# Attention values taken per unit instead of per pair of heads, with five buffers for turned weights instead of six

## The reference

```python
o_cmp = einsum(masked_softmax(q k_cmp^T), v_cmp)   # 31 compressed keys
o_sel = einsum(masked_softmax(q k_sel^T), v_sel)   # causal, branch 0 in the kernel
o_win = einsum(masked_softmax(q k_win^T), v_win)   # causal, branch 1
o = g0 * o_cmp + g1 * o_sel + g2 * o_win           # 16 heads of 64, 4 groups of keys
return o @ w_out
```

## Time and profile before

| | |
|---|---|
| median of 3 runs | 1592.23 us (1592.12 to 1593.16) |
| the profiled execution's own time | 1593.16 us |
| its span, first to last instruction | 1591.4 us |
| PE busy over the span | 1527.1 us (96%) |
| DVE, ACT, POOL busy | 1109.3, 689.9, 309.6 us |
| granted PE clock, mean | 0.99 of full speed |

### The profile page before, as it was taken

The page is one execution under the profiler, slowest core; times in us unless marked ns, Lnnn a source line. Parts: engine busy times, 40 slices in busy tenths (PEclk is TensorE's granted clock), DMA queues, the critical chain, the costliest instruction groups (busy, mean ns, idle before and its releaser), DMA issues. The chain is left out here.

```text
span 1591.4 us, 20732 instructions
## 1 busy us (share of the span) xinstructions
PE 1527.1 (96%) x8107; PEld 1258.5 (79%) x8107; DVE 1109.3 (70%) x1607; ACT 689.9 (43%) x1175; POOL 309.6 (19%) x237
## 2 busy tenths in 40 slices
PE   4898999999999999989999999999999999999998
PEld 3687898888888897867777888888888987766677
DVE  6688888898889763359885685656634814788775
ACT  3432552322314544337774541322233524778551
POOL 0122112233222000039872011111100011000210
PEclk9899999999999999989999999999999999999999
DMA  9575246669575314230000255433432231211101
GB/s 332 201 249 185 80 152 238 232 199 329 197 273 180 106 32 157 89 105 2 2 1 28 80 200 170 145 134 122 142 106 93 71 109 66 78 67 53 54 1 53
DMA packets 106743, 203.33 MB, mean 128 GB/s; under 512 B 6025, under 2 KB 11414, under 8 KB 106646
## 3 DMA queue, kind: packets, MB, share of 16 engines
q1 hardware_dynamic: 106646, 202.01, 36.9%
HBM read 199.90 MB, written 2.10 MB: 127 GB/s over the span
## 5 line engine op out<-in xcount | busy, mean ns | idle before, releaser
L722 ACT ACTIVATE WH<-RAW 128x2048 fp32r<-128x2048 f32 (+1 forms) x112 | 210.1, 1886 | 362.1 <-DMA RAW<-in_ff_w_in_dram 218.9
L1219 DVE TENSOR_TENSOR WL<-RAW,WH 128x2048 fp32r<-128x2048 f32 (+1 forms) x107 | 276.5, 2604 | 128.9 <-ACT WH L722 128.1
L486 POOL PARTITION_ALL_REDUCE MROW<-MACC x30 | 142.2, 4740 | 596.9 <-DVE MACC L1253 511.3
L2055 PE MATMUL PS<-WH,HIDh 128*128 128x512 f32 (+1 forms) x576 | 218.4, 379 | 5.9 <-DVE HIDl L1537 4.9
L2055 PE MATMUL PS<-WL,HIDh 128*128 128x512 f32 (+1 forms) x576 | 218.2, 379 | 0.0
L2055 PE MATMUL PS<-WH,HIDl 128*128 128x512 f32 (+1 forms) x576 | 218.2, 379 | 0.0
L2055 PE MATMUL PS<-HTh,WH 128*128 128x512 f32 (+1 forms) x520 | 202.4, 389 | 0.0
L2055 PE MATMUL PS<-HTl,WH 128*128 128x512 f32 (+1 forms) x520 | 202.4, 389 | 0.0
L2055 PE MATMUL PS<-HTh,WL 128*128 128x512 f32 (+1 forms) x520 | 202.3, 389 | 0.0
L1253 DVE SCALAR_TENSOR_TENSOR MACC<-MRAW,CS,MACC 128x512 f32<-128x512 f32 x182 | 136.9, 752 | 9.2 <-DMA MRAW<-in_ada_w_dram 1.0
L2012 PE MATMUL PS<-HTh,WH 128*128 128x256 f32 (+1 forms) x384 | 124.8, 325 | 6.7 <-ACT SG L1098 2.5
(11 more groups left out here) (325 smaller groups left out, 2935.2 us busy)
## 6 DMA issues: line engine op xcount, KB each, us to landing
MRAW<-in_ada_w_dram SPq DMA_DIRECT2D x46, 1024.0 KB, 7.3
RAW<-in_ff_w_in_dram SPq DMA_DIRECT2D x32, 1024.0 KB, 5.3
RAW<-in_ff_w_out_dram SPq DMA_DIRECT2D x32, 1024.0 KB, 5.0
RAW<-in_w_in_dram SPq DMA_DIRECT2D x16, 1024.0 KB, 5.3
MRAW<-in_w_ada_dram SPq DMA_DIRECT2D x12, 1024.0 KB, 9.0
RAW<-in_a_w_in_dram SPq DMA_DIRECT2D x8, 1024.0 KB, 9.7
MRAW<-in_kv_ada_w_dram SPq DMA_DIRECT2D x8, 1024.0 KB, 6.1
RAW<-in_kv_w_dram SPq DMA_DIRECT2D x6, 1024.0 KB, 5.1
```

The source lines that it names most:

```text
L486: pool.partition_all_reduce(MROW[:], MACC[:], P, RADD).then_inc(m_red, 1)
L722: act.activation(WH[:, wslot(u), 0:width(u)], RAW[:, u % 4, 0:width(u)], ACT.Copy).then_inc(w_hi, 1)
L1219: dve.tensor_tensor(WL[:, u % 4, 0:width(u)], RAW[:, u % 4, 0:width(u)], WH[:, wslot(u), 0:width(u)].bitcast(F32), ALU.subtract).then_inc( ...
L2055: mm = pe.matmul(po, a, b_, start=(k == 0 and i == 0), stop=(k == KT - 1 and i == len(ops) - 1), skip_group_check=len(ops) > 3)
```

## The change

`values` goes unit by unit: at i = 3 it takes the units i = 1, 3 and 2, and at i = 6 the units 4, 6 and 5. Each unit belongs to one head, and all its matmuls come one after the other. The near tile of head 0 (unit 2) is thereby multiplied at i = 3 and no longer at i = 6. Each stage now has 10 matmuls; before it was 8 and 12 where S is even and 6 and 14 where it is odd. Which matmuls there are does not change.

PT is a ring of five buffers over the rows of all superunits, so that a copy waits for the `values` that read the row five before it. The copy of i = 5 goes from ACT to DVE. The constants MD, IDB and MCM lie behind the PT, PBC and PTC buffers in on-chip memory, where the sixth PT was, and no longer ahead of them.

```diff
+    PT = [scratch(f"PT{i}", [P, 512]) for i in range(5)]
 ...
     MD, IDB = scratch("MD", [P, P], BF16), scratch("IDB", [P, P], BF16)
     MCM = scratch("MCM", [P, TT, 32], BF16)
 ...
-        return PT[row(u) % 6] if u % PER else PTC[u // PER % 2]
+        return PT[row(u) % 5] if u % PER else PTC[u // PER % 2]
 ...
-        return u % PER not in (3, 6)
+        return u % PER in (0, 1, 2, 4)
 ...
-        return 3 * (u // PER) + (1, 2, 3, 2, 3, 3, 3)[u % PER]
+        return 3 * (u // PER) + (1, 2, 2, 2, 3, 3, 3)[u % PER]
 ...
-        return u - PER if u % PER else u - 2 * PER
+        if u % PER == 0:
+            return u - 2 * PER
+        r = row(u) - 5
+        return PER * (r // 6) + r % 6 + 1 if r >= 0 else -1
 ...
-                pairs = ((1, 0, (u - 2, u)),) if i == 3 else ((1, 1, (u - 2, u)), (0, 0, (u - 4, u - 1)),
-                                                              (0, 1, (u - 4, u - 1)))
-                for blk, br, of in pairs:
-                    for kt in range(qts[blk] + 1):
-                        c_ = P * kt + (P * (qts[0] + 1) * br if blk == 0 else 0)
-                        for h in range(2):
-                            mm = pe.matmul(head(blk, h), VT[:, br, kt, HD * g:HD * g + HD],
-                                           turned_of(of[h])[:, c_:c_ + P], start=False,
-                                           stop=(br == 1 and kt == qts[blk]), skip_group_check=True)
+                for v in (u - 2, u, u - 1):
+                    S, i, pair, qts, blk, br, e, L = unit(v)
+                    for at_, br_ in parts(v):
+                        for kt in range(qts[blk] + 1):
+                            c_ = at_ + P * kt
+                            mm = pe.matmul(head(blk, e), VT[:, br_, kt, HD * g:HD * g + HD], turned_of(v)[:, c_:c_ + P],
+                                           start=False, stop=(br_ == 1 and kt == qts[blk]), skip_group_check=True)
```

More of the change, by code:

```diff
@@ L187, in program @@
     VC = scratch("VC", [P, GROUPS, 2 * HD])
+    assert w_at[0] <= o_w + 16384
+    w_at[0] = o_w + 16384
+    PT = [scratch(f"PT{i}", [P, 512]) for i in range(5)]
+    PBC = [scratch(f"PBC{i}", [P, P]) for i in range(2)]
+    PTC = [scratch(f"PTC{i}", [P, 2 * P]) for i in range(2)]
     MD, IDB = scratch("MD", [P, P], BF16), scratch("IDB", [P, P], BF16)
     MCM = scratch("MCM", [P, TT, 32], BF16)
[L191 to L195, removed]
     second = [at(n, [P, 4, T], F32, o) for n, o in (
```

## The result

| | before | after |
|---|---|---|
| median | 1592.47 us (1592.12 to 1593.16, 4 runs) | 1609.22 us (1606.83 to 1609.85, 4 runs) |
| ratio | | 1.0102, 95% interval 1.0085 to 1.0119 |
| profiled execution, span | 1593.16, 1591.4 us | 1608.31, 1606.6 us |

The change costs 16.7 us by the medians and 15.2 us by the two profiled spans. The forecast was 1614.4, in a range of 1600 to 1619: the right way and inside, but by the medians the loss is a quarter smaller than the forecast 22.2 us. Each ratio further down is taken against runs of the kernel before from the same session as the experiment (medians 1593.14 us for e1 to e4, 1593.19 for e5 to e8, 1593.01 for e9 and e10).

The account below looks back on a forecast made before the run. PE was taken to bound the attention: +24.4 us for values in one-head runs, less 1.3 and 0.9 us gained back, made +22.2 us, a median of 1614.4 us (chance 55%). Range 1600 to 1619 us, its own 1612 to 1619.

Parts of the forecast that it names:

- PE sets the pace, and values of one head take twice the time: Attention body: PE bounds; one head's matmul alone takes 0.218 us, and two of different heads share that time.
- One slot saved at each change of head, +24.4 us: Stages of values: a new run starts with the last matmul before it; 17 slots of 0.218 us a superunit against 10.
- the bounds: Cost of the stages of values: +10.5 us if the halves run fully apart, +34.9 us if nothing overlaps.
- the rival of halves running apart: Stages of values: a stage lasts as long as its busier head; +9.2 us, 1601.4 us; chance 25%.
- the case to which I gave 7%: Stages of values: the queue passes over one or two more matmuls than forecast; 1602 to 1614 us; chance 7%.
- the first rival: Stages of values: the halves of the array run apart; +9.2 us, 1601.4 us; chance 25%.
- What PE gains back, 2.2 us: PE fills its 1.3 us wait for POOL near the end and 0.9 us of gaps between 711 and 750 us.
- The ring, 0: Unit 6's copy on DVE newly waits for the stage i = 3 just before: 0, up to 2 us with the margin gone.
- The copy on DVE, 0: Unit 5's copy adds 8.8 us to DVE, hidden by PE: 0, at most 8.8 us if that cover were gone.
- No overlap: Stages of values: one-head runs go wholly one after another; +32.7 us, 1624.9 us; chance 7%.
- A gain through ACT: Transpositions of units 3 and 4 on wait less for ACT's copies; some 2 us faster, 1590 us; chance 3%.
- the 2.2 of the prediction: Stage of values at i = 6: expected to last 2.2 us if the forecast is right.

Follow-up runs that it names:

- e1: Kernel before with only the new order of the values, six PT buffers and unit 5's copy on ACT: 1607.35 us, ratio 1.0089.
- e4: Kernel before with all tiles of keys of one head ahead of the other's, within each block and branch: 1601.23 us, ratio 1.0054.
- e5: Kernel before with only the copy of unit 5 moved to DVE: 1595.04 us, ratio 1.0014.
- e8: Kernel before with both stages of values of a superunit joined into one, placed at t - 15 in PE's order: 1610.19 us, ratio 1.0107.
- e9: Kernel before with unit 6's copy moved from DVE to ACT, so DVE copies unit 3 alone: 1597.41 us, ratio 1.0028.
- e10: Kernel before with unit 3's copy moved from DVE to ACT, so DVE copies unit 6 alone: 1597.81 us, ratio 1.0033.
- e3: Kernel before with heads alternating every two matmuls instead of every one: 1595.23 us, ratio 1.0012.
- e2: Changed kernel with the far tile's two heads alternating matmul by matmul and the near unit alone at the end: 1600.65 us, ratio 1.0050.
- e6: Changed kernel with the old order of the values put back, keeping the ring of five and unit 5's copy on DVE: 1594.27 us, ratio 1.0009.

## Why the prediction was right, and where it was off

*PE sets the pace, and values of one head take twice the time.* Right. The stretches after are full, and the experiments that only reorder the values lengthen PE's stages by what a count of slots says.

*One slot saved at each change of head, +24.4 us.* This is the term that was mis-sized. Measured from the stages it is +17.4. The forecast had 17 slots a superunit; two slots saved at each of three changes make 14, or 14.0 us over the attention. The rest, 3.4 us, comes in two halves. In the eight stages i = 3 with S odd, head 0 alone needs 7 slots and not the 6 of this count, 8 x 0.218 = 1.7 us. And a run that sets in anew loses 0.05 us, twice in the stages i = 3 with S even and once in each stage i = 6, 8 x 0.10 + 16 x 0.05 = 1.6 us. What failed is the choice between the bounds: I counted a deeper overlap at nothing because no row showed it. The earlier trace rows has three records passing one that waited; how many may wait it does not show. So the rows gave my step as the least overlap and left a deeper one open, and I took the least as the likeliest. The truth lay between my forecast and the rival of halves running apart, in the case to which I gave 7%. e3 and e4 exclude both neighbours.

So the time lies below the 1612 to 1619 that I gave for my own mechanism, and inside the whole range only because that reached down to the first rival. The direction and the engine were reasoned; that the time fell inside owes more to the width of the range than to the sum.

*What PE gains back, 2.2 us.* Right in size: 17.4 of stages against 15.2 of span. Its parts were not as I had them, so that the sum agrees is in part luck. POOL's 1.30 us went, but 0.81 came back by the ring, and the small waits in the body, which I took only from the stretches ahead of 750 us, gave 0.11 us in every superunit, 1.8 in all.

*The ring, 0.* Right in the body, wrong at the end. I had counted the two scores and two transpositions that lie between a stage i = 3 and the need for unit 6's copy. In the last superunit there are no scores left and the next stage follows at once, so that cover was gone. A cover must be looked for at the last turn of a loop as well.

*The copy on DVE, 0.* Right in this kernel, since the longer stages hide it; alone it costs some 2 us (e5: 1.9 by the medians, interval 0.6 to 3.7).

*Rivals.* Halves running fully apart: out, by e4. No overlap: out, by all stages. A gain through ACT: out; e9 and e10 show that ACT's copies do matter to PE, but in the other direction only, when there are more of them, and e5 shows no gain from fewer, though there DVE's lateness could hide a small one.

The medians differ by 16.7 us and the profiled times by 15.15, because the profiled execution of before lay 0.7 over its median and that of after 0.9 under its own. What stays open is whether the bound on passing is three records, or a time, or a number of instructions (each record has its load beside it), since all records of values here have 128 columns.

## What to carry to other kernels

Where two matmuls use half of the array's columns each, write them alternately; what the order of the program puts in long runs of one half overlaps only at the seams, at a price that the duration of each stage shows directly (the same 24 records took 1.53 us alternating and 2.02 in runs of up to four matmuls). Equal counts of matmuls in two stages are no balance if the partners stand in different stages: count for each half, and the larger is the least that the stage can take. Before giving a copy to the engine with more free time, look whether the pieces in its queue leave room at the moment when it is needed.

## What the runs showed of the hardware

A half of the array lets the other pass, but not without bound. With alternation by one or two matmuls both halves are filled from the start; with runs of three or four the second half starts when three records of the first still wait. The stages of the changed kernel, e2 and e4, four kinds of stage in each, follow this to 0.02 us, and those of e3 to 0.06. The three rest on the changed kernel and e4: two or four in their place miss the stages of 2.02 us by 0.10 or more. The Trainium skill, "TensorE: Matmul & The Clock Gate", part 3, has matmuls strictly in program order; the start of head 1's records ahead of three waiting ones of head 0 speaks against that (a stage i = 6 of 2.02 us, where strict order of whole matmuls gives the 2.2 of the prediction), and the measurement decides.

The attention begins with a stretch at half clock (granted clock 0.50, the level of 1.2 GHz of 2.4), whose length differs between the profiled executions. In the kernel before, the changed one, e5 and e6 PE had stood almost still in the microsecond before it (busy 0.12 us or less), and was busy for most of it until the clock rose. The stretch ended near 705 us before (mean 0.76 from 697 to 711 us) and in the changed kernel just before 711 (0.52). There it cost nothing that shows: the first values start at 718.18 us against 718.36. In e5 and e6 it lasted until 716 and 715 us, and the first values came at 721.80 and 720.66, 3.4 and 2.3 us later. That is about what these two executions have over their medians (3.4 and 2.4). The clock is a likelier cause of it than the copies, but no run separates them.
